# A two-layer mixer and two-layer expert network on one core: ScalarE's copies of a round put behind its next exponentials, one modulation piece a round, a total and two PSUM banks moved in the grouped rounds

## The reference

```python
for i in range(2):
    mod = silu(c) @ ada_w[i] + ada_b[i]              # 1024 x 6144: shifts, scales and gates
    sh1, sc1, g1, sh2, sc2, g2 = split(mod, 6)
    h = x * (1 + sc1) + sh1
    if i == 0: y = neighbourhood_attention(h @ w_qkv, rpb) @ w_o     # 16 heads, biased softmax
    else:      y = grouped_attention(rope(norm(h @ w_qkv))) @ w_o    # 16 query, 4 key heads
    x = layer_norm(ALPHA * x + (1 + g1) * y)
    h = x * (1 + sc2) + sh2
    y = experts(h)                  # 2 of 32 experts a token; three weights of 2 MB an expert
    x = layer_norm(ALPHA * x + (1 + g2) * y)
```

## Time and profile before

| what | value |
|---|---|
| median of 3 runs | 1589.41 us (1588.25 to 1590.89) |
| the profiled execution | 1588.65 us, its span 1586.9 us |
| TensorE busy | 1397.0 us, 88% of the span |
| VectorE busy | 568.5 us, 36% |
| ScalarE busy | 219.4 us, 14% |
| moved by DMA | 533.32 MB, mean 336 GB/s |
| chain that ended last | PE 64%, DMA 25%, DVE 7%, ACT 2% |

### The profile page before, as it was taken

One profiled execution on the slowest core, in us unless ns is written; L12 is line 12 of the kernel. 1 busy time (PEld: TensorE's weight loads), 2 busy tenths in 40 slices (PEclk: granted clock), 3 DMA queues, 4 the chain that ended last, 5 costly groups with the idle time before them and its releaser, 6 DMA issues.

```text
span 1586.9 us, 28389 instructions
## 1 busy us (share of the span) xinstructions
PE 1397.0 (88%) x12800; PEld 885.6 (56%) x12800; DVE 568.5 (36%) x1230; ACT 219.4 (14%) x578; POOL 87.9 (6%) x95
## 2 busy tenths in 40 slices
PE   7999999998998989789789788868998797897795
PEld 4885488577885555345445344447654554554442
DVE  3696569556835101101101115684211011111113
ACT  2230214011432000000000002332100000000000
POOL 3100111000003000000000001100200000000000
PEclk9999999999998999889989898989899998999999
DMA  9656846776856999999999998346799999999995
GB/s 346 235 196 237 299 163 209 249 287 226 301 223 259 427 426 426 427 427 426 427 428 424 425 372 295 105 160 267 295 425 427 427 425 427 425 428 425 426 419 199
DMA packets 96856, 533.32 MB, mean 336 GB/s; under 512 B 5184, under 2 KB 7424, under 8 KB 73168
## 3 DMA queue, kind: packets, MB, share of 16 engines
q1 hardware_dynamic: 92992, 519.40, 81.2%
q0 software_dynamic: 3728, 11.95, 2.2%
HBM read 530.28 MB, written 1.05 MB: 335 GB/s over the span
## 4 chain that ended last, share of the span: by engine, by line
PE 64%; DMA 25%; DVE 7%; ACT 2%; issue 1%; SPq 1%; DVEq 0%; ACTq 0%
PE bk L429 25%; DMA AR<-in_moe_w_down 24%; PE bk L892 18%; PE bk L926 8%; PE bk L610 3%; PE bk L936 3%; PE bk L425 3%; DVE AR L1011 2%; ACT AR L1817 1%; PE bk L654 1%; PE bk L639 1%; DVE mpart L1019 1%; SPq L2300 1%; DMA ring<-in_w_in 1%; DMA ring<-in_ada_w 1%
## 5 line engine op out<-in xcount | busy, mean ns | idle before, releaser
L892 PE MATMUL bk<-ring,AR 128*32 128x128 f32 x5120 | 307.8, 409 | 4.2 <-DVE AR L1016 4.2
L892 PEld LDWEIGHTS bk<-ring,AR 128*32 128x32 f32 x5120 | 192.4, 127 | 103.0 <-DVE AR L1016 5.3
L1011 DVE TENSOR_TENSOR AR<-bk,AR 128x128 f32<-128x128 f32 (+2 forms) x106 | 41.3, 389 | 539.2 <-ACT AR L1817 467.0
L429 PE MATMUL bk<-ring,AR 128*128 128x256 f32 (+2 forms) x736 | 211.7, 445 | 9.0 <-DVE lsum L1011 3.0
L1817 ACT ACTIVATE AR<-bk 128x512 f32<-128x512 f32 (+4 forms) x178 | 71.9, 422 | 1014.2 <-PE bk L892 789.8
L926 PE MATMUL bk<-ring,AR 128*32 128x512 f32 x656 | 163.6, 719 | 37.0 <-DMA ring<-in_moe_w_down 37.0
L926 PE MATMUL bk<-AR 128*32 128x512 f32 x368 | 148.9, 715 | 46.7 <-DMA AR<-in_moe_w_down 45.9
L892 PE MATMUL bk<-AR 128*32 128x128 f32 x3072 | 187.3, 410 | 0.0
L429 PEld LDWEIGHTS bk<-ring,AR 128*128 128x128 f32 x736 | 140.5, 193 | 75.0 <-issue 54.4
L429 PE MATMUL bk<-AR,ring 128*128 128x256 f32 (+1 forms) x832 | 172.9, 367 | 7.1 <-DVE diag L1011 5.4
L429 PEld LDWEIGHTS bk<-AR,ring 128*128 128x128 f32 x832 | 149.0, 192 | 28.0 <-DVE diag L1011 5.8
(11 more groups left out here) (152 smaller groups left out, 968.6 us busy)
## 6 DMA issues: line engine op xcount, KB each, us to landing
ring<-in_moe_w_gate SPq DMA_DIRECT2D x48, 2048.0 KB, 24.6
ring<-in_moe_w_down SPq DMA_DIRECT2D x36, 2048.0 KB, 28.6
ring<-in_moe_w_up SPq DMA_DIRECT2D x32, 2048.0 KB, 20.2
AR<-in_moe_w_up SPq DMA_DIRECT2D x32, 2048.0 KB, 29.2
ring<-in_ada_w SPq DMA_DIRECT2D x24, 2048.0 KB, 11.0
AR<-in_moe_w_down SPq DMA_DIRECT2D x20, 2048.0 KB, 29.1
AR<-in_moe_w_gate SPq DMA_DIRECT2D x16, 2048.0 KB, 15.8
ring<-in_w_in SPq DMA_DIRECT2D x12, 2048.0 KB, 13.0
```

What stands on the lines that cost most here:

```text
L429: ins = eng.matmul(o, l, r, start=i == 0, stop=i == len(pairs) - 1)
L892: ins = eng.matmul(o[32 * f:32 * f + 32, 128 * m:128 * m + 128], XG[u][:, c, 32 * j:32 * j + 32], w[:, c, f::4], start=c == 0, stop=c == N ...
L1011: return eng.tensor_tensor(o, a, b, op)
```

## The change

It has six parts. (1) In ScalarE's `attend`, `settle()` moves from the end of round i to behind the numerators of round i+1, for all three kinds of attention. (2) `Sa`, a Silu of a gate, moves a round earlier in the hybrid layers. (3) In `NA_SIDE` one piece of modulation (`+`, `+`) moves from round 2 to round 6, so each of rounds 1 to 6 has one piece. (4) `NA_LOADS` and the arena's three numbers change, and with them the slots; SP's order of pieces stays. (5) `t20` moves from round 3's fill to between `q00` and `K0`, and `x20` from round 5's side work to round 0. (6) The three fill banks of the late grouped rounds (7, 0, 1) come one round sooner, at round 7.

```diff
-FILL = tuple((("qk0",), ("qk1",) + one, ("v0",), ("v1", "tot"), ("s0",), ("s1", "Sd"), ("a0",), ("a1", "Sc"),
-              ("b1", "tot", "Sa"), ("b0",), ("g1", "tot"), ("g0",), ("spat", "tot", "Sb")) for one in ((), ("tot",)))
+FILL = tuple((("qk0",), ("qk1",) + one, ("v0",), ("v1", "tot"), ("s0",), ("s1", "Sd"), ("a0",), ("a1", "Sc", "Sa"),
+              ("b1", "tot"), ("b0",), ("g1", "tot"), ("g0",), ("spat", "tot", "Sb")) for one in ((), ("tot",)))
...
 NA_ROUNDS = (("t13", "k2", "k3", "q2", "q3"), ("t14", "v00", "v10", "k4", "k5", "p04"),
              ("t15", "v01", "v11", "k6", "k7", "p06"), ("t16", "v02", "v12"), ("t17", "v03", "v13"),
              ("p14", "g0", "g1", "g2", "g3"), ("p16", "l", "o00"), ("o01",), ("o02",), ("o03",))
-NA_SIDE = ((), ("x13", "+", "+"), ("x14", "+", "+", "+", "+"), ("x15", "+", "+"), ("x16", "+", "+"), ("x17", "+", "+"),
-           ("m",), ("l", "o00"), ("o01",), ("o02", "o03", "s"))
-
-NA_LOADS = ((2, 399), (0, 406), ("ada", 13, 383), (3, 441), (4, 435), ("ada", 14, 400), (1, 485), ("ada", 15, 417),
-            (5, 471), ("ada", 16, 431), ("ada", 17, 445), ("ada", 18, 455), ("ada", 19, 466),
-            ("wo", 0, 528), ("wo", 1, 535))
-GQA_ROUNDS = (("q01",), ("r10",), ("q11",), ("r01", "t20"), ("t21",), ("r11",),
+NA_SIDE = ((), ("x13", "+", "+"), ("x14", "+", "+"), ("x15", "+", "+"), ("x16", "+", "+"), ("x17", "+", "+"),
+           ("m", "+", "+"), ("l", "o00"), ("o01",), ("o02", "o03", "s"))
+
+NA_LOADS = ((2, 378), (0, 378), ("ada", 13, 355), (3, 426), (4, 408), ("ada", 14, 374), (1, 466), ("ada", 15, 393),
+            (5, 448), ("ada", 16, 409), ("ada", 17, 426), ("ada", 18, 439), ("ada", 19, 452),
+            ("wo", 0, 498), ("wo", 1, 505))
+GQA_ROUNDS = (("q01",), ("r10",), ("q11",), ("r01",), ("t21",), ("r11",),
               ("o00",), ("l", "o01"), ("o02", "t22"), ("o03",))
-GQA_SIDE = (("v10",), ("w10",), ("v01", "+", "w01"), ("+",), ("v11", "+", "w11"), ("x20", "+"), ("x21", "n", "+"), ("m", "+", "o00"),
+GQA_SIDE = (("x20", "v10"), ("w10",), ("v01", "+", "w01"), ("+",), ("v11", "+", "w11"), ("+",), ("x21", "n", "+"), ("m", "+", "o00"),
             ("l", "o01"), ("o02", "x22", "o03", "s"))
 GQA_LOADS = ((2, 14), (0, 39), (1, 52), ("ada", 20, 8), ("ada", 21, 53), ("wo", 0, 115), ("wo", 1, 123), ("ada", 22, 70),
              ("ada", 23, 85))
...
                         put(("out", l, f) if f in (0, 1) else ("in", l, f), RING)
             for *f, when in NA_LOADS:
                 put(("wo", 0, f[1]) if f[0] == "wo" else ("ada", f[1]) if f[0] == "ada" else ("qkv", 0, *f), RING, when)
-            for k, when in enumerate((519, 521, 541)):
+            for k, when in enumerate((486, 487, 510)):
                 age[RING + k] = when
             now[0] = 1000
             for i in range(DEPTH):
...
                     norm_cols(1, t)
                 for f in ("k0", "k1", "q00", "K0", "K1", "q10", "r00"):
                     unit(f)
+                    if f == "q00":
+                        total(20, next_bank())
                 fill_bank[0] = [7]
                 todo = list(GQA_ROUNDS)
 
                 def fill():
-                    if len(todo) == 2:
+                    if len(todo) == 3:
                         fill_bank[0] = [7, 0, 1]
                     for f in todo.pop(0):
                         if f[0] == "t":
...
                                 s.tell(ins, sem("exp"), nth(tag, p))
                             else:
                                 s.step(ins)
+                    if i:
+                        settle()
                     if i >= 3 and tag in TAG:
                         outputs(tag, i - 3)
                     if i >= 2:
...
                                 s.wait_ge(*filled("o", tag, j - 2))
                             free(act(ET[u][:, 4 * b:4 * b + 4, :], bank("pT", tag, j, b)[:, :].rearrange("p (i k) -> p i k", i=4),
                                      ACT.Copy), "pT", tag, j, b)
-                    settle()
+                settle()
                 if tag in TAG:
                     outputs(tag, n - 1)
 
```

## The result

The changed kernel took 1573.2 us (median of 4 executions, 1571.46 to 1573.99), the kernel before beside it 1589.29 (median of 4, 1588.25 to 1590.89): a ratio of 0.9896, 95% interval 0.9879 to 0.9914, or 16.1 us faster. The prediction was 19.0 us and 1570.4, with a range of 1564.5 to 1579. The profiled execution took 1573.72 us, its span 1571.9.

What follows compares the result with a forecast made beforehand. Weight streaming was taken to bound expert stages, TensorE's matmuls the hybrid layers, VectorE the grouped rounds. Savings of 7.6 and 11.4 us sum to 19.0: 1569.6, or 1570.4 us as median, range 1564.5 to 1579.

Steps and rivals of the forecast that it cites:

- Hybrid layers, 0 with bounds of 0 and -0.5: Both hybrid layers: TensorE is almost always busy, so ScalarE's saved table loads gain 0, at most 0.5 us.
- Neighbourhood, -7.6: Neighbourhood rounds: moving a modulation piece out of round 2 saves 5.39 and 2.37 us, less 0.2, 7.6 in all.
- The stall of 5.39 and the slow stretch of 2.37: TensorE at `k6`: its 5.39 us idle goes whole, and the 64 matmuls behind it become 2.37 us shorter.
- The price of 0.2: Neighbourhood rounds 6 and 4: the moved piece or a later copy might make VectorE late; bounds 0 and 5.96 us.
- Grouped rounds, -11.4: Grouped rounds: VectorE sets the pace; its shorter chain and the earlier `l` and `o01` save 11.35 us.
- Start of the chain -3.7: Grouped rounds: group 1's maxima start on VectorE at 1008.5 instead of 1012.23 us, with the total in front counted.
- Up to `l` -7.45: Grouped rounds: earlier chain start, `x20` off the chain and fewer breaks bring `o00` and `l` 7.45 us earlier.
- `l` to `o01` -3.1: Grouped rounds: with banks a round sooner, `o01` follows `l` 0.3 us behind instead of 3.41, saving 3.1.
- `o01`'s slow half -0.8: Grouped rounds: `o01` took 5.28 us against 3.72 for `o00`; half of the 1.56 was counted, 0.8 saved.
- `x20` and the total in front: Grouped rounds: `x20` leaving VectorE's chain saves 1.8 us; `t20` ahead of everything adds about 1.1.
- `r11`'s longer stall: Grouped rounds: `r11` stands about 6 us until `x21` frees its bank; the 6.63 us stall before `t21` moves there.
- the six rounds with an exposed copy: Rival, chance 0.04: first six grouped rounds each expose a copy behind numerators, 23 us lost against 19 saved, about 1593.

Runs made afterwards that it cites:

- near_only: The kernel before with only the neighbourhood's part: modulation piece moved from round 2 to 6, new load times and slots; 1583.7 us, ratio 0.9955.
- grouped_only: The kernel before with only the grouped part: total 20 in front, `x20` in round 0, three fill banks a round sooner; 1583.35 us, ratio 0.9953.
- side_only: The changed kernel with the old `NA_LOADS` and ages, so the modulation piece is moved but the slots are not; 1571.9 us, ratio 0.9878.
- l_bank0: The changed kernel with only the order of the three fill banks altered, to 0, 1, 7; 1571.54 us, ratio 0.9881.
- after_again: The changed kernel measured once more, unaltered; 1571.7 us, ratio 0.9886 to the kernel before.
- banks_late: The changed kernel with its three fill banks given one round later, as before the change; 1574.93 us, ratio 0.9916.
- total_back: The changed kernel with `t20` back in round 3, `x20` back in round 5 and no total in front; 1573.17 us, ratio 0.9897.
- order_only: The kernel before with only ScalarE's new order: numerators ahead of copies in all attentions, `Sa` a round earlier; 1585.73 us, ratio 0.9969.
- order_grouped: The kernel before with ScalarE's new order and the grouped part together, the neighbourhood's part left as before; 1578.28 us, ratio 0.9925.
- swap_busy: The kernel swap plus extra identity transposes in TensorE's waits ahead of the hybrid layers' and neighbourhood's first products; 1567.18 us, ratio 0.9850.
- swap: The changed kernel with `r11` ahead of `t21` and the three fill banks in the order 0, 1, 7; 1568.19 us, ratio 0.9862.

## Why the prediction was right

It was right in its main steps and missed one term. That the first pair's median fell short of the forecast by only 2.9 us is in part luck: the grouped rounds gave 1.1 us more than forecast in the profile and the neighbourhood 0.4 less, while the hybrid layers, put at 0, took 4.5 back.

- **Hybrid layers, 0 with bounds of 0 and -0.5: missed.** ScalarE's part of this step holds: four table loads fewer (574 instructions on ScalarE, 578 before), and near_only and grouped_only show that a long hybrid stretch needs no change there. What failed is the bound. I looked for what the change moves, and not for how much TensorE's rate varies by itself behind the waits at 12 and 165 us. The same two products took 18.31 to 21.28 and 18.11 to 19.81 us over the profiles, 4.8 us between the shortest and the longest hybrid part (318.65 and 323.44). The profile that I worked from had both short; of the other eleven without transposes two had (side_only and l_bank0). So the term is a spread, and a change of 0 was the wrong claim for any single pair. Most of the gap between 19.0 and the 16.1 measured first can be this: after_again gave 18.45.
- **The advice on the clock.** The Trainium skill ("TensorE: Matmul & The Clock Gate", "What's actually happening") puts the slow start at under 1% of a typical kernel, advises against fitting a model to it, and says also that it varies from run to run of the same kernel. The trace agrees with both, here for stretches behind waits inside the kernel: 4.8 us of 1570 are 0.3%. That is under 1%, but more than the 3.2 us that I took as the least that a measurement of this kernel tells from no change, so the variation bears on this case more than the advice.
- **Neighbourhood, -7.6: -7.18.** The stall of 5.39 and the slow stretch of 2.37 went whole, as two terms of their own: near_only saves 7.93. The price of 0.2 was 0.7, and it lies at another place than the two that I named: not VectorE in round 6 but the bank of the gate rows, which ScalarE now frees behind its numerators. The weights of the moved piece, expected at 374, came nearly in time (a wait of 0.31 us). What I didn't foresee is that with the new slots the weights of round 2's own piece are late (5.59 us, 1.46 in side_only with the old ones), without reaching TensorE. side_only shows that the slots, which I let pass at no cost, had no gain either.
- **Grouped rounds, -11.4: -12.54.** Start of the chain -3.7: measured -3.91. Up to `l` -7.45: -7.80. `l` to `o01` -3.1: -3.13, and by itself in banks_late 3.14. `o01`'s slow half -0.8: -1.61, the whole of it; this is the term that was mis-sized. I had kept half because TensorE would stand 3 us ahead of `l`; it stood 1.08. `x20` and the total in front: -1.8 and +1.1 forecast, a net 0.7; total_back gives 0.95 with a short first product, order_only against order_grouped 1.67, as two small waits for scores go as well. I gave `r11`'s longer stall no price because VectorE doesn't wait for it; l_bank0 and swap_busy show 2.0 us to be had there, since TensorE's work up to `l` set the end. The waits for ScalarE's copies were 2.57 and 1.46 us, against 2.5 and 1.5.
- **The experts**: 503.85 and 503.87 us. Over all the profiles this stretch was 503.8 to 505.8, so it scatters by up to 2 us, without a relation to the change that I can see. The two longest (swap 505.72, total_back 505.82) are those whose next stage began with the short product, so a part of the scatter only moves over the border between the stages.
- **The rivals.** Of the ways to be slower, the six rounds with an exposed copy didn't happen: two were exposed, and VectorE wanted those scores later. They came about because the copy stands behind the numerators in ScalarE's program: at 1008.98 us, right behind the last numerator of 1008.53, while group 2's scores waited until 1009.64. The Trainium skill ("TensorE: Matmul & The Clock Gate", "Architectural detail") calls ScalarE's queue strictly first in, first out, and this trace agrees.

What stays open: whether filling TensorE's waits removes the long hybrid stretches (two of two profiles were short, against three of twelve), what sets them at all, and whether the first one is the clock (the record says 1.00 there) or something else. The sum of the attention stages' savings, 19.7 us, is 1.3 more than the second measured difference, 3.6 more than the first; the hybrid spread is of that size, but no run fixes its mean.

## What to carry to other kernels

Put the work of an in-order engine that the pace-maker waits for ahead of its copies, and then see which bank or result the copies now hold back; here that cost 0.7 us in the neighbourhood rounds and brought 5 in the grouped ones. Where two results in a row share a bank, follow the second one's wait: a bank order of 0, 1, 7 in place of 7, 0, 1 and a transpose ahead of a total were worth 3.2 us more. And before a few microseconds are explained by a change, profile the same code again, and compare first the stretches that no edit touches.

## What the runs showed of the hardware that was not expected

- The same 48 matmuls took 18.31, about 20 or 21.28 us in identical instructions: 18.31 behind waits of 1.75 to 1.83 us, the others behind 1.56 to 1.70 and behind 1.90. At the second place, behind 1.96 to 1.98 us, they took 18.1 or 19.8, and nothing between.
- The granted clock of the record was 1.00 from 14 to 18 us while matmuls began at 4 in 2 us, the rate that goes with 0.50 at 169 to 171 us.
- 48 matmuls of 512 columns at the start of the grouped stage took 22.8 to 23.4 us in twelve profiles and 20.8 in two. In the changed kernel the granted clock was 0.50 until 966.4 us, 8 us into the stage; in swap it was 0.93 already from 961.5 to 963.5, 4 to 6 us into it.
- The wait of 0.45 us at the gate rows cost 0.7 in after and side_only and 1.56 more in both kernels with transposes ahead. In grouped_only rows near there ran at a granted clock of 0.50 (434 to 436 us) with TensorE busy all the time before.
